# A hybrid attention layer with a seven-product feed-forward on one core: sums of x formed tile by tile, weight sums ahead of low parts, three down steps prepared early

## The reference

```
mix = (sigmoid(ga) * (oa @ w_br_a) + sigmoid(gb) * (ob @ w_br_b)) @ w_out
x   = x + rms_norm(mix, norm_mix_post)
h   = rms_norm(x, norm_ffn_pre)
gate, up = split(h @ w_gate_up)
y   = x + rms_norm((silu(gate) * up) @ w_down, norm_ffn_post)
```

## Time and profile before

| what | value |
|---|---|
| median of 3 runs | 1585.75 us (1585.61 to 1586.13) |
| profiled execution, its time | 1586.32 us |
| its span, first to last instruction | 1584.5 us |
| mean granted TensorE clock, of full speed | 0.99 |
| TensorE busy | 96% of the span |
| VectorE, ScalarE, GpSimd busy | 50%, 44%, 37% |
| feed-forward part and down projection begin | about 826 and 1306 us into the span |

### The profile page before, as it was taken

One profiled execution on the slowest core, in us unless ns is written; L12 is line 12 of the kernel. 1 busy time (PEld: TensorE's weight loads), 2 busy tenths in 40 slices (PEclk: granted clock), 3 DMA queues, 4 the chain that ended last, 5 costly groups with the idle time before them and its releaser, 6 DMA issues. The chain is left out here.

```text
span 1584.5 us, 28317 instructions
## 1 busy us (share of the span) xinstructions
PE 1521.7 (96%) x10334; PEld 1403.9 (89%) x10334; DVE 793.0 (50%) x1326; ACT 697.7 (44%) x1529; POOL 583.0 (37%) x440
## 2 busy tenths in 40 slices
PE   6999999999999999998997899999999999999998
PEld 6899999999898998996776899999999996778886
DVE  6574473655737468546458333333333343353533
ACT  6354364564647457434334233333333333353433
POOL 2102111011020110531202777777777754434342
PEclk9999999999999999999998999999999999999999
DMA  6112112111021222444212222222222218666572
GB/s 194 48 58 62 56 42 71 58 56 58 31 67 59 62 75 88 142 143 166 81 67 67 81 81 80 75 71 70 74 72 80 81 62 278 182 230 184 183 246 88
DMA packets 169885, 157.15 MB, mean 99 GB/s; under 512 B 24328, under 2 KB 146736, under 8 KB 169808
## 3 DMA queue, kind: packets, MB, share of 16 engines
q1 hardware_dynamic: 162896, 147.46, 30.7%
q10 hardware_dynamic: 6912, 8.65, 1.5%
HBM read 122.38 MB, written 33.70 MB: 99 GB/s over the span
## 5 line engine op out<-in xcount | busy, mean ns | idle before, releaser
L1727 ACT ACTIVATE w_hi<-w_raw 128x512 fp32r<-128x512 f32 x88 | 55.6, 632 | 231.3 <-POOL w_raw L1669 231.3
L1958 PE MATMUL m_ya<-f_xc,w_hi 128*128 128x264 f32 x704 | 145.7, 289 | 8.6 <-ACT f_temps L1738 4.7
L1672 POOL TENSOR_TENSOR w_lo<-w_raw,w_hi 128x512 fp32r<-128x512 f32 x88 | 113.6, 1291 | 104.9 <-ACT w_hi L1727 104.9
L903 POOL TENSOR_TENSOR w_lo<-w_raw,w_hi 128x1024 fp32r<-128x1024 f32 x19 | 46.2, 2437 | 278.9 <-ACT w_hi L931 278.9
L1958 PE MATMUL m_yb<-f_xc,w_hi 128*128 128x264 f32 x704 | 144.0, 285 | 3.1 <-DVE f_xc L2114 3.1
L1958 PEld LDWEIGHTS m_ya<-f_xc,w_hi 128*128 128x128 f32 x704 | 116.8, 192 | 9.3 <-issue 9.3
L1958 PEld LDWEIGHTS m_yb<-f_xc,w_hi 128*128 128x128 f32 x704 | 116.0, 189 | 3.7 <-DVE f_xc L2114 3.7
L1230 DVE TENSOR_TENSOR_SCAN b_fail<-b_fail 128x128 f32<-128x128 f32 (+8 forms) x72 | 93.2, 1294 | 38.7 <-ACT b_fail L959 38.6
L329 POOL TENSOR_TENSOR w_lo<-w_raw,w_hi 128x1024 fp32r<-128x1024 f32 x15 | 36.2, 2411 | 180.3 <-ACT w_hi L365 180.3
L1958 PE MATMUL m_ya<-f_xc,w_lo 128*128 128x264 f32 x352 | 100.9, 287 | 0.0
L1958 PE MATMUL m_yb<-f_xc,w_lo 128*128 128x264 f32 x352 | 100.6, 286 | 0.0
(11 more groups left out here) (329 smaller groups left out, 4712.8 us busy)
## 6 DMA issues: line engine op xcount, KB each, us to landing
f_raw<-in_w_down_dram SPq DMA_DIRECT2D x44, 512.0 KB, 3.7
w_raw<-in_w_in_dram SPq DMA_DIRECT2D x32, 512.0 KB, 3.9
act_scratch<-x_whole SPq DMA_DIRECT2D x22, 528.0 KB, 3.8
f_raw<-in_w_gate_up_dram SPq DMA_DIRECT2D x22, 512.0 KB, 5.4
f_raw_odd<-in_w_gate_up_dram SPq DMA_DIRECT2D x22, 512.0 KB, 5.4
f_raw_odd<-in_w_down_dram SPq DMA_DIRECT2D x22, 512.0 KB, 3.7
m_gate<-gate_scratch SPq DMA_DIRECT2D x16, 528.0 KB, 4.5
gate_scratch<-a_gst ACTq DMA_DIRECT2D x24, 176.0 KB, 1.9
```

The costliest lines, as they stand in the source:

```text
L903: pool.tensor_tensor(w_lo[:, SLOT[j % NU], :, :], w_raw[:, 1, SLOT[j % NU], :, :], w_hi[:, SLOT[j % NU], :, :].bitcast(F32), ALU.subtract) ...
L1672: pool.tensor_tensor(w_flat(m, 1), whole, w_flat(m, 0).bitcast(F32), ALU.subtract).then_inc(w_rest, 1)
L1727: act.activation(w_flat(m, 0), whole, ACT.Copy).then_inc(w_rounded, 1)
L1958: last = pe.matmul(BANK[m][c][:, 0:CH], w_slot(m, w)[:, k, :], left(m, x, k, c), start=(m < 3 and k == 0 and n == 0), stop=(k == 3 and n = ...
```

## The change

The diff, cut to what changes the work or its order (renamed lists, semaphores' declarations and the matching counts left out):

```diff
-                x_sums = [sb(same, f"f_x_sums{n}", [P, 2, 4, TH]) for n in range(5)]
+                x_sums = sb(same, "f_x_sums", [P, 2, 4, TH])
...
+            def xspot(n, c):
+                return {1: x_whole[1][:, 4:8, t1(c)], 2: x_whole[0][:, 4:8, t1(c)],
+                        3: x_whole[0][:, 0:4, t2(c)], 4: x_whole[1][:, 0:4, t2(c)]}[n]
...
             def xsum(n, c):
-                return x_sums[n][:, 1, :, t1(c)]
+                return xspot(n, c) if n else x_sums[:, 1, :, t1(c)]
...
-                for q in range(2):
+                for q in range(4):
                     load_down(q)
                 store_unit(NIT - 1, 1)
-                for q in range(2, STEPS):
+                for q in range(4, STEPS):
...
+                def w_head(it, e):
+                    w_add(it, e, 0)
+                    w_add(it, e, 1)
+                    w_low(it, e, 0)
+                    w_add(it, e, 2)
+                    for m in range(1, 5):
+                        w_low(it, e, m)
+                    w_add(it, e, 5)
+
+                def w_parts(it, e):
+                    w_head(it, e)
+                    w_add(it, e, 6)
+                    w_low(it, e, 5)
+                    w_low(it, e, 6)
...
-                w_parts(0, 0, range(NW - 1))
+                w_head(0, 0)
+                w_low(0, 0, 5)
...
+                pool.tensor_tensor(x_whole[1][:, k2, at1], s_raw[:, k1, two], s_raw[:, k2, two], ALU.add).then_inc(s_ready, 1)
+                pool.tensor_tensor(x_whole[0][:, k2, at1], s_raw[:, k1, one], s_raw[:, k2, one], ALU.add).then_inc(s_ready, 1)
+                pool.tensor_tensor(x_whole[0][:, k1, at2], s_raw[:, k1, one], s_raw[:, k1, two], ALU.subtract).then_inc(s_ready, 1)
+                pool.tensor_tensor(x_whole[1][:, k1, at2], s_raw[:, k2, two], s_raw[:, k2, one], ALU.subtract).then_inc(s_ready, 1)
...
-                pool.wait_ge(x_rest, 7)
-                w_parts(0, 0, (NW - 1,))
+                pool.wait_ge(x_rest, 8)
+                w_add(0, 0, 6)
+                w_low(0, 0, 6)
...
                 def x_round(n, c):
-                    act.wait_ge(x_sum[c], n + 1)
+                    if n == 0:
+                        act.wait_ge(x_sum, c + 1)
+                    else:
+                        act.wait_ge(h_lo, 2 * (NBLK + c))
+                        act.wait_ge(s_ready, 8)
...
-                def step(it, e, ahead):
+                def step(it, e, ahead, head=True):
...
+                    if head:
                         copy_v(it, e)
+                        w_round(it, e, 6)
+                    if ahead:
+                        for m in range(3):
+                            w_round(*nxt, m)
+                    for c in range(2):
+                        gate_2(it, e, c)
+                    if ahead:
+                        w_round(*nxt, 3)
                     else:
+                        for q in range(3):
+                            down_round(q)
+                    for c in range(2):
+                        copy_up(it, e, c)
                     if ahead:
                         w_round(*nxt, 4)
                         w_round(*nxt, 5)
                     for c in range(2):
                         gate_1(it, e, c)
-                    if ahead:
-                        w_round(*nxt, 6)
...
-                    if t in (3, 4, 5):
-                        act.wait_ge(o_lo_done, KT)
-                        for m in range(2 * t - 6, 2 * t - 4):
-                            w_round(0, 0, m)
...
+                    if t in (2, 3, 4):
+                        act.wait_ge(o_lo_done, KT)
+                        for m in range(2 * t - 4, 2 * t - 2):
+                            w_round(0, 0, m)
                     if t == NBLK:
                         x_round(0, 0)
+                        x_round(1, 0)
                 act.wait_ge(xn_ready, NT)
                 copy_v(0, 0)
-                for n, c in ((1, 0), (0, 1), (1, 1), (2, 0), (2, 1), (3, 0)):
+                for n, c in ((0, 1), (1, 1), (2, 0), (2, 1), (3, 0), (3, 1)):
                     x_round(n, c)
                 for c in range(2):
                     gate_2(0, 0, c)
-                for n, c in ((3, 1), (4, 0)):
-                    x_round(n, c)
+                for c in range(2):
+                    x_round(4, c)
+                w_round(0, 0, NW - 1)
                 for c in range(2):
                     copy_up(0, 0, c)
-                x_round(4, 1)
-                w_round(0, 0, NW - 1)
-                for e in range(2):
-                    step(0, e, True)
+                for m in range(3):
+                    w_round(0, 1, m)
+                for c in range(2):
+                    gate_1(0, 0, c)
+                copy_v(0, 1)
+                for m in range(3, NW):
+                    w_round(0, 1, m)
+                step(0, 1, True, False)
...
-                    if g and f < 3:
-                        square(3 * g - 3 + f)
+                    if g and f == 0:
+                        square(3 * g - 3)
+                        square(3 * g - 2)
+                    if g and f == 1:
+                        square(3 * g - 1)
...
-                pe.wait_ge(h_lo, 2 * NT)
+                pe.wait_ge(h_lo, 2 * NT - 1)
...
+                def xs(c):
+                    dve.tensor_tensor(xsum(0, c), xspot(1, c), xspot(3, c), ALU.add).then_inc(x_sum, 1)
...
+                            elif plain:
+                                dve.tensor_copy(x_whole[1][:, other, fcols(i)], turns[1]).then_inc(h_lo, 1)
                             else:
-                                dve.tensor_copy(x_whole[1][:, other, fcols(i)], turn).then_inc(h_lo, 1)
+                                x21, x22 = (x_whole[n][:, 0:4, fcols(i + 4)] for n in range(2))
+                                dve.wait_ge(h_lo, 2 * t - 2)
+                                dve.tensor_tensor(x_whole[1][:, 4:8, fcols(i)], x21, x22, ALU.add)
+                                dve.tensor_tensor(x21, turns[0], x21, ALU.subtract)
+                                dve.tensor_tensor(x22, x22, turns[1], ALU.subtract)
+                                x12 = x_whole[0][:, 4:8, fcols(i)]
+                                dve.tensor_tensor(x12, turns[0], x12, ALU.add).then_inc(h_lo, 1)
...
                         if t == NBLK:
                             dve.wait_ge(h_lo, 2 * NBLK)
-                            xs(0, 0)
+                            xs(0)
...
                     if last:
-                        for q in range(2):
+                        for q in range(3):
                             low(q)
...
-                xs(0, 1)
-                x_low(1, 0)
-                xs(1, 1)
+                xs(1)
+                x_low(0, 1)
+                x_low(1, 1)
                 for c in range(2):
                     v_add(0, 0, c, 1)
...
+                    if g and f == 0:
+                        normalise(3 * g - 3)
+                        normalise(3 * g - 2)
+                        add(3 * g - 3)
+                    if g and f == 1:
+                        add(3 * g - 2)
+                        normalise(3 * g - 1)
+                    if g and f == 2:
+                        add(3 * g - 1)
...
+                def weigh(half):
+                    cols = slice(half * HALF, (half + 1) * HALF)
+                    dve.tensor_tensor(yn[:, 2, cols], mixed(p, half), post[:, cols], ALU.mult).then_inc(evicted, 1)
...
+                    dve.scalar_tensor_tensor(yn[:, 2, cols], yn[:, 2, cols], stat[:, p, 4:5], x1_back[:, 2, cols],
+                                             ALU.mult, ALU.add).then_inc(y_ready, 1)
```

110 lines of the change are left out of this document (41 added, 69 removed).

## The result

The kernel after took 1569.45 us (median of four runs, 1565.85 to 1570.81) against 1585.94 for the kernel before, 16.5 less. The ratio on record is 0.9885, 95% interval [0.9873, 0.9897]; it is not the quotient of these two medians, which is 0.9896. So the change is 1.0 to 1.2% faster. Forecast were 1565.5, a ratio of 0.987, and 1560 to 1572. The profiled execution took 1570.46 with a span of 1568.7, 15.8 less than before's 1584.5.

What follows compares the result with a forecast made beforehand. TensorE was busy 1521.7 of 1584.5 us, so only its idle time and half-clock stretches could be won. Gains of 2.1 + 11.7 + 4.5 + 0.9 + 1.0 = 20.2, off the median 1585.75, gave 1565.5; range 1560 to 1572.

Steps and rivals of the forecast that it cites:

- main case: Whole kernel: all gains and new waits as worked out, 1565.5 us, within 1562 to 1568.5; chance 0.60.
- point 6: Down projection: three steps prepared early remove the wait of 3.03 and the low clock behind it; gain 4.5 us.
- Roundings moved: Output projection: unit 0's roundings behind the square roots remove two transpose waits of 1.03; gain 2.1 us.
- Small sums: Projection: x sums made tile by tile on VectorE cost nothing for three tiles, delay the last transposes 1.9 us.
- To unit 1's first product: Behind the projection: GpSimd starts 1.0 us sooner, TensorE starts at 856.5, waiting about 0.5 instead of 2.98.
- GpSimd as the bound of unit 1: Unit 1: 16 GpSimd instructions leave TensorE one wait of about 4 us; unit 2 starts 11.7 us sooner.
- The steady loop: Feed-forward units: GpSimd's chain takes 11.9 us, its reader is due after 14.6; slack 2.7, gain zero.
- the rival on the other side: Feed-forward units: chain over 2.7 us later makes TensorE wait in every unit; at 5 us, 1611; chance 0.05.
- Group changes: Down projection's group changes: bank freed 3 us sooner, step 24 comes 0.2 to 1.1 late; gain 0.9 us.
- last tile: Kernel end: one multiplication before the norm, one beside the root, then two fused steps; gain 1.0 us.
- The rule weighed: VectorE with two SBUF inputs and GpSimd lock a shared port pair per instruction; by it 1568, otherwise 1565.5.
- the collision: Unit 1: first four GpSimd instructions each meet VectorE and pay 0.7; wait 2.5 us longer, 1568; chance 0.10.

Runs made afterwards that it cites:

- second profile of after: The kernel after run again with no edit; 1568.20 us, ratio 0.9888.
- late sums: Kernel after with the sums of x formed after the projection again, in VectorE's and ScalarE's order of the kernel before; 1573.02 us, ratio 0.9912.
- one input in PSUM: Kernel after with VectorE's low parts of the fifth sum reading one operand from PSUM, that result not computed; 1567.36 us, ratio 0.9874.
- the pair of runs with the alternation: Kernel after with GpSimd alternating sum and low part from unit 1: 1579.83 us; also with ScalarE's seventh rounding ahead of V's copies: 1574.13 us.
- the kernel with alternation: Kernel after with GpSimd making each sum and at once its low part from unit 1 on, nothing else edited; 1579.83 us, ratio 0.9952.

## Why the prediction was right, point by point

The time lies 4 us above the forecast and inside the range of 1560 to 1572, but above the 1562 to 1568.5 of the main case, in the part that was left to the rivals. The sign of each part was as forecast, and the mechanism too, but for ScalarE's and VectorE's share in point 6. In the frame of the profiles the forecast was a span of 1584.5 - 20.2 = 1564.3, and 4.4 more were measured: 1.8 ahead of the third tile's transposes, -0.5 in the projection, 2.5 behind it, 0.7 in the rest (0.15 in the second profile of after), which adds up to 4.5. Some 2.7 of that is clock that kernels with the same work up to there did not lose: 1.5 in the stretch from 752 on and 1.15 behind unit 1's first product.

1. *Roundings moved.* About right in size: both waits of 1.03 are gone, and with late sums the projection was 2.5 shorter than before (69.56 for 72.05), forecast 2.1. The reason was half of it, as the run with the roundings put back showed: one wait goes by GpSimd's order (the second sum ahead of the first low part), one by the place of the roundings.
2. *Small sums.* Forecast +1.9 for the last transposes and nothing for three tiles. With late sums the projection was 1.8 shorter, and no earlier transposes waited in after: right.
3. *To unit 1's first product.* Forecast GpSimd's start 16.7 us behind the last transposes, measured 852.34 - 835.49 = 16.85; TensorE's start of unit 1 forecast 24.1 behind them, measured 25.6. Most of the 1.5 is contention: with one input in PSUM it was 24.3.
4. *GpSimd as the bound of unit 1.* **This is the term that was mis-sized.** Forecast were 16 instructions at 1.27 "plus 0.5 where a rounding sits behind two copies of V and 0.3 for contention". The 0.3 for contention were 1.2 on the two sums alone, and with one input in PSUM the sixth product starts 1.2 sooner at equal clock. The 0.5 were 1.89, because the second copy of V waits for a product that ran at low clock; where the clock was 1.00 the same rounding cost 0.31, and the sixth product came 1.15 sooner. The two make up the miss: with neither, in the run with one input in PSUM, the sixth product started 42.9 behind the last transposes and unit 2 50.4, as forecast (879.2 - 836.3 = 42.9 and 50.3). The third sum of unit 2 ended 43.8 behind the last transposes, forecast 41.3 (877.6 - 836.3); unit 2 started 52.8 behind them, forecast 50.3 (886.6 - 836.3). Against the 64.0 of before that is a gain of 11.2 where 13.7 were forecast: 2.5 too much. That "this wait replaces those removed" and hangs on the sigmoid behind unit 2's third rounding was right (3.36 for "about 4"), as was its low clock (7.45 from 880.81 to unit 2, forecast 5.8 + 1.6).
5. *The steady loop.* Right: 20.4 a unit. But the rival on the other side was nearer than its 0.05 suggests. The pair of runs with the alternation showed that the mechanism I gave for it, ScalarE's seventh rounding behind V's copies, does lengthen the loop by 0.28 a unit, if GpSimd's order isn't changed with it. The slack of 2.7 was worked out for the new order, and only for that.
6. *Down steps early.* Forecast 4.5; with the steps put back the part from unit 2 on grew by 3.2 to 3.7, of which the wait is 3.3 + 0.2 less the 0.56 that step 5 waits now (it was named as next late). Right for the wait. The 1.5 of low clock behind it were there in the kernel before and not in the run with the steps put back, so they are neither shown to be gained nor refuted. The credit for ScalarE's and VectorE's part was wrong: they give nothing.
7. *Group changes and* 8. *last tile.* Forecast 0.9 and 1.0. The wait at the group change went from 1.54 to 0.64, the pair of adds at the end is gone; together they measured 1.9 to 2.4.

**The rule weighed.** The forecast named 1568 as the sum by the Trainium skill's rule on the port pair that VectorE and GpSimd share (SBUF — State Buffer, SBUF: two separate sides), and 1565.5 by the row alone. What the rule says of the condition and of the lock agrees with the trace: with one of VectorE's inputs in PSUM both delays are gone, and with two in SBUF each instruction ended 1.1 to 1.2 after the other engine's. The row of 854.46 in the kernel before fits too: VectorE's sum ended at 856.43, 1.11 after GpSimd's of 854.03 had. So it was not a single case, as the 1565.5 took it. As a rival the collision was carried at 0.10, with 2.5 us on unit 1. Unit 2 was indeed 2.5 later than forecast, but only 1.2 of that is the collision and the rest is clock, so that the median lies nearer to 1568 than to 1565.5 is in part chance.

What was never in the forecast is the clock of stretches that are alike in both kernels. Half clock behind short waits was there or not in kernels with the same work. It made the stretch of the projection 1.5 us longer, the way to the sixth product of unit 1 1.15, and the way from there to unit 2 1.5 to 2.4. So two profiles can differ by 3 us with no cause in the change. The same is open for the 3 us by which the first column of the table varies.

## What to carry to other kernels

When an engine alternates between its own work and the low part that needs another engine's answer, putting the next sum ahead of the low part takes the round trip (0.74 each here) out of the chain, and it also decides how much delay the other engine's queue may add. When the list of waits names an engine, read what stands ahead of the releasing instruction in the queue of the engine behind it: here VectorE was named, ScalarE's order was the cause, and moving unit 1's sigmoids ahead of three roundings (4.3) was worth no less than the forming of the sums in the projection (3.3 net). Ahead of a forecast of a few us, count the short waits that may or may not be followed by half clock, since each was worth 1.2 to 2.4 here. And before a difference between two profiles is put down to an edit, compare the granted clock of the same stretch: half of what the run with one input in PSUM seemed to give was clock.

## What the runs showed of the hardware that was not expected

- The granted clock behind a wait of 1.3 to 3.4 us differs between kernels with the same instructions up to there: 0.57 in one profile and 1.00 in another behind the wait of 1.3 in the projection, 0.63 and 1.00 behind the 1.9 in unit 1, in windows of 4 us at the same place of the program.
- A low part of 128x1056 on VectorE with two SBUF inputs, beside GpSimd sums of 128x512: the pair took 4.23 us, and GpSimd's pair 3.73. With one input in PSUM they took 2.40 and 2.72. Both engines lose, because they take turns by whole instructions: VectorE's two ended 1.12 and 1.11 after GpSimd's had, and GpSimd's next 1.16 after VectorE's.
- A loop can lose 1.4% of TensorE's matmuls with no entry in the list of waits: the kernel with alternation did. The count of matmuls in a window of equal length showed it, and so does the distance of one instruction from the same one a unit later (20.69 for 20.40).
